# Layer norms by token tile, and a feed-forward net's first unit by token tile

## The reference, cut to what matters

```python
for l in range(DEPTH):                       # DEPTH = 2, ALPHA = (2 * DEPTH) ** 0.25
    x = layer_norm(ALPHA * x + 0.5 * swiglu(x, ffn_w1[l, 0], ffn_w2[l, 0]), ln_g[l, 0], ln_b[l, 0])
    mix = hybrid_mixer(x, ...)
    x = layer_norm(ALPHA * x + mix, ln_g[l, 1], ln_b[l, 1])
    x = layer_norm(ALPHA * x + 0.5 * swiglu(x, ffn_w1[l, 1], ffn_w2[l, 1]), ln_g[l, 2], ln_b[l, 2])

def layer_norm(x, g, b):
    mu = mean(x);  var = mean((x - mu) ** 2)
    return (x - mu) * rsqrt(var + 1e-5) * g + b

def swiglu(x, w1, w2):                       # w1: 1024 x 5632, w2: 2816 x 1024
    g, u = split(x @ w1, 2)
    return (silu(g) * u) @ w2
```

## Time and profile before

| | us |
|---|---|
| time before, median of 3 runs | 1828.71 (1828.14 to 1828.81) |
| the profiled execution | 1828.23 |
| its span (first to last instruction) | 1826.2 |

### The profile page before, as it was taken

One profiled execution on the slowest core, in us unless ns is written; L12 is line 12 of the kernel. 1 busy time (PEld: TensorE's weight loads), 2 busy tenths in 40 slices (PEclk: granted clock), 3 DMA queues, 4 the chain that ended last, 5 costly groups with the idle time before them and its releaser, 6 DMA issues.

```text
span 1826.2 us, 27995 instructions
## 1 busy us (share of the span) xinstructions
PE 1779.8 (97%) x10838; PEld 1567.5 (86%) x10838; DVE 1386.7 (76%) x1543; ACT 989.5 (54%) x953; POOL 60.0 (3%) x99
## 2 busy tenths in 40 slices
PE   9999999999999999999999999999999889999998
PEld 8888899998888888888999988888899668787786
DVE  7655786857778775557868577887768878879988
ACT  6555465633544454444655335444433636869984
POOL 1000000000000000000000000000100010000001
PEclk9999999999999999999999999999999899999999
DMA  7555454564677655554555637775534009989994
GB/s 264 202 192 198 156 179 175 187 252 139 231 276 269 237 184 184 185 194 152 187 186 198 233 124 262 264 286 198 174 116 139 24 8 355 365 323 398 423 381 173
DMA packets 58423, 395.79 MB, mean 217 GB/s; under 512 B 7016, under 2 KB 7392, under 8 KB 12752
## 3 DMA queue, kind: packets, MB, share of 16 engines
q1 hardware_dynamic: 48800, 350.31, 52.8%
q0 software_dynamic: 9504, 44.00, 7.3%
q10 hardware_dynamic: 16, 0.01, 0.0%
HBM read 386.94 MB, written 7.36 MB: 216 GB/s over the span
## 4 chain that ended last, share of the span: by engine, by line
PE 73%; DVE 15%; ACT 4%; issue 3%; DVEq 3%; ACTq 1%; DMA 0%; SPq 0%
PE ps L2207 14%; PE ps L2191 7%; PE ps L2193 7%; PE ps L2192 7%; PE ps L2206 7%; PE ps L2307 3%; PE ps L2308 3%; PE ps L2311 3%; DVE wlo L2670 3%; DVE wlo L1743 2%; PE ps L2204 2%; DVE mod L2798 2%; PE ps L990 2%; PE ps L992 1%; PE ps L991 1%
## 5 line engine op out<-in xcount | busy, mean ns | idle before, releaser
L2670 DVE TENSOR_TENSOR wlo<-raw,whi 128x2048 fp32r<-128x2048 f32 x235 | 536.0, 2290 | 188.5 <-ACT whi L2495 186.4
L2495 ACT ACTIVATE whi<-raw 128x2048 fp32r<-128x2048 f32 x235 | 449.3, 1912 | 279.2 <-PE ps L2193 104.0
L2207 PE MATMUL ps<-xT,whi 128*128 128x512 f32 x1232 | 439.4, 396 | 0.0
L2206 PE MATMUL ps<-xT,wlo 128*128 128x256 f32 x1232 | 344.0, 279 | 0.0
L2207 PEld LDWEIGHTS ps<-xT,whi 128*128 128x128 f32 x1232 | 231.2, 188 | 47.5
L2191 PE MATMUL ps<-xT,whi 128*128 128x256 f32 x912 | 258.2, 283 | 0.0
L2192 PE MATMUL ps<-xT,whi 128*128 128x256 f32 x912 | 258.1, 283 | 0.0
L2193 PE MATMUL ps<-xT,wlo 128*128 128x256 f32 x912 | 258.1, 283 | 0.0
L2206 PEld LDWEIGHTS ps<-xT,wlo 128*128 128x128 f32 x1232 | 232.3, 189 | 8.8 <-DVE xT L2689 1.0
L2519 ACT ACTIVATE rest<-ps 128x512 f32<-128x512 f32 x88 | 52.8, 600 | 241.8 <-PE ps L2207 241.8
L2191 PEld LDWEIGHTS ps<-xT,whi 128*128 128x128 f32 x912 | 175.1, 192 | 0.0
(11 more groups left out here) (589 smaller groups left out, 3358.9 us busy)
## 6 DMA issues: line engine op xcount, KB each, us to landing
raw<-stream SPq DMA_DIRECT2D x236, 1024.0 KB, 4.8
raw<-experts SPq DMA_DIRECT2D x64, 1024.0 KB, 7.7
mod<-experts SPq DMA_DIRECT2D x32, 1024.0 KB, 7.6
adaraw<-ada POOLq DMA_DIRECT2D x24, 1024.0 KB, 5.1
yd<-lnrow POOLq DMA_DIRECT2D x7, 512.0 KB, 6.9
lnrow<-ln_g POOLq DMA_DIRECT2D x6, 512.0 KB, 4.7
lnrow<-ln_b POOLq DMA_DIRECT2D x6, 512.0 KB, 7.2
yd<-lnrow POOLq DMA_DIRECT2D x10, 256.0 KB, 6.5
```

The source lines that it names most:

```text
L2206: nc.tensor.matmul(bank(b, T), wl, xThi[:, k, :], start=False, stop=False)
L2207: return nc.tensor.matmul(bank(b), wh, both, start=False, stop=k == KD - 1)
L2495: act_fn(whi[:, slot, :], raw[:, slot, :], ACT.Copy).then_inc(hi_done, 1)
L2670: v.tensor_tensor(wlo[:, slot, :], raw[:, slot, :], whi[:, slot, :].bitcast(F32), ALU.subtract).then_inc(lo_done, 1)
```

## The change

The norm does all its steps for tile 0, then all for tile 1, with a root of its own for each tile; `mv_done` and `std_done` count tiles. `PIECES` becomes [(0, 0), (0, 1), (1, 0), (1, 1)]. In the norms ahead of a net the low parts of the first two pieces stand behind the two sums of tile 1. ScalarE loads its square root table ahead of the norm and takes one root per tile; between the tiles it splits the weight unit that it split ahead of the norm before; VectorE's weight splits stay behind the norm. In the last step of a net, hidden values are made, split and counted by tile, so `hid_done` and `hlo_done` count one more per net, and `last_rows` waits by tile and always takes the third bank late. `first_unit` multiplies all chunks for tile 0, then for tile 1, with products of 256 and 128 columns, and four fillers between. `first_turned_unit` turns the two pieces of tile 0, runs ten fillers, and begins its products after the third piece. The fillers right behind `last_rows` are gone.

```diff
-NORM_FILL, MERGE_FILL, H1_FILL, H1_TURN_FILL, H2_FILL, TURN_FILL = 20, 18, 25, 8, 17, 5
+MIX_FILL, TILE_FILL, H1_FILL, H1_TURN_FILL, H2_FILL, TURN_FILL = 10, 4, 25, 8, 17, 5
...
-        PIECES = [(0, 0), (1, 0), (0, 1), (1, 1)]
+        PIECES = [(0, 0), (0, 1), (1, 0), (1, 1)]
...
+            def tile_product(slot, tile, k, b, i):
+                c = k * 256 + tile * P
+                wh, wl = whi[:, slot, c:c + P], wlo[:, slot, c:c + P]
+                sl = slice(i * P, (i + 1) * P)
+                both = bank(b).rearrange("p (a t) -> p a t", t=T)[:, :, sl]
+                low = bank(b, T + i * P, T + (i + 1) * P)
+                if k == 0:
+                    nc.tensor.matmul(both, wh, xT[:, k, :, sl], start=True, stop=False)
+                    return nc.tensor.matmul(low, wl, xThi[:, k, sl], start=False, stop=False)
+                nc.tensor.matmul(low, wl, xThi[:, k, sl], start=False, stop=False)
+                return nc.tensor.matmul(both, wh, xT[:, k, :, sl], start=False, stop=k == KD - 1)
...
             def first_unit(rnd, slot, n):
-                for j in range(3):
-                    turn_piece(n, j)
-                for half in range(2):
-                    pe.wait_ge(xTlo_done, n * 4 + (2 * half + 2))
-                    if half == 0:
-                        weights_ready(rnd, slot)
-                    for tile in range(2):
-                        for k in range(4 * half, 4 * half + 4):
-                            last = wide_product(slot, tile, k, tile)
-                        if (half, tile) == (0, 0):
-                            turn_piece(n, 3)
+                turn_piece(n, 0)
+                turn_piece(n, 1)
+                weights_ready(rnd, slot)
+                for i in range(TT):
+                    if i == 1:
+                        keep_busy(TILE_FILL)
+                        turn_piece(n, 2)
+                        turn_piece(n, 3)
+                    for half in range(2):
+                        pe.wait_ge(xTlo_done, n * 4 + (2 * i + half + 1))
+                        for tile in range(2):
+                            for k in range(4 * half, 4 * half + 4):
+                                last = tile_product(slot, tile, k, tile, i)
                 last.then_inc(used, 1)
...
             def first_turned_unit(rnd, slot, b, n):
-                for j in range(3):
-                    turn_piece(n, j)
-                pe.wait_ge(xThi_done, n * 4 + 2)
+                turn_piece(n, 0)
+                turn_piece(n, 1)
+                keep_busy(MIX_FILL)
+                turn_piece(n, 2)
+                pe.wait_ge(xThi_done, n * 4 + 3)
                 weights_ready(rnd, slot)
                 high_products(slot, 0, range(4), outs[0], False)
                 turn_piece(n, 3)
...
             (last_rows)
-                    if bank_no == 0:
+                    if bank_no % 2 == 0:
                         weights_ready(rnd, slot)
-                        pe.wait_ge(*before[j])
+                        pe.wait_ge(*before[j][i])
...
-                if third_first:
-                    part(0, 2)
...
             (ScalarE, at a norm; split_piece is one turn of the old split_stream)
-                norm(l * 3)
-                split_stream(l * 3 + 1)
+            def split_stream(n, base, o):
+                norm_root(n - 1, 0)
+                split_piece(n, 0)
+                split_piece(n, 1)
+                turn(base, o)
+                norm_root(n - 1, 1)
+                split_piece(n, 2)
+                split_piece(n, 3)
...
             (VectorE, norm)
+                def root(i):
+                    dve.wait_ge(std_done, n * TT + i + 1)
+                    v.reciprocal(rstd[:, i, :], std[:, i, :])
+                    dve.drain()
+                    v.tensor_scalar(newt[:, i:i + 1], rstd[:, i, :], rstd[:, i, 0:1], var[:, i, 0:1], ALU.mult, ALU.mult)
+                    dve.drain()
+                    v.scalar_tensor_tensor(rstd[:, i, :], newt[:, i:i + 1], 1.5, rstd[:, i, :], ALU.add, ALU.mult)
+                    dve.drain()
+
+                def normed(i):
+                    moments(i).then_inc(mv_done, 1)
+                    dve.drain()
+                    v.tensor_scalar(var[:, i, :], mv[:, i, 1:2], LN_EPS, -0.5, ALU.add, ALU.mult)
+                    ...
+                    centred(i, 0)
+                    last = centred(i, 1)
+                    ...
+                    root(i)
+                    for h in range(2):
+                        ins = scaled(i, h)
+                        if then != "block2":
+                            ins.then_inc(x_done, 1)
+
                 summed(0, 0)
                 summed(0, 1)
+                normed(0)
                 summed(1, 0)
+                if then == "ffn":
+                    stream_lo(n + 1, 0)
                 summed(1, 1)
+                if then == "ffn":
+                    stream_lo(n + 1, 1)
+                normed(1)
...
             (VectorE, last_step of a net; high is banks 2 and 3, first part)
+                    def tile_hidden(i):
+                        sl = slice(i * P, (i + 1) * P)
+                        ...
+                        v.tensor_tensor(hid[:, 0, :, sl], high[:, :, sl], rest[:, 1, :, sl], ALU.add)
+                        dve.drain()
+                        v.scalar_tensor_tensor(hid[:, 0, :, sl], sil[:, :, sl], 0.5, hid[:, 0, :, sl], ALU.mult,
+                                               ALU.mult).then_inc(hid_done, 1)
+                    ...
+                    tile_hidden(0)
+                    tile_hidden(1)
+                    tile_lo(0)
+                    tile_lo(1)
```

More of the change, by code:

```diff
@@ L2315, in rows_unit, with last_rows @@
                 last.then_inc(used, 1)
-            def last_rows(units, parts, before, third_first):
+            def last_rows(units, parts, before):
                 def part(j, bank_no):
@@ L2337, in last_rows @@
                 part(0, 1)
-                if third_first:
-                    part(0, 2)
                 part(1, 0).then_inc(y0_done, 1)
                 part(1, 1).then_inc(y0_done, 1)
-                if not third_first:
-                    part(0, 2)
+                part(0, 2)
                 part(1, 2).then_inc(y0_done, 1)
@@ L2430, in _ @@
                 ffn(lay, l * 2, l * 3)
-                keep_busy(NORM_FILL)
                 for hf in range(2):
@@ L2751, in norm @@
-                centred(1, 0)
-                dve.drain()
-                dve.wait_ge(std_done, n + 1)
-                v.reciprocal(rstd[:, :, 0], std[:, :, 0])
-                dve.drain()
-                for i in range(TT):
-                    v.tensor_scalar(newt[:, i:i + 1], rstd[:, i, :], rstd[:, i, 0:1], var[:, i, 0:1], ALU.mult, ALU.mult)
-                dve.drain()
-                v.scalar_tensor_tensor(rstd[:, :, 0], newt[:, 0:TT], 1.5, rstd[:, :, 0], ALU.add, ALU.mult)
-                dve.drain()
+                if then == "ffn":
+                    stream_lo(n + 1, 1)
@@ L2773, in norm @@
                     return
-                def piece(j):
-                    scaled(*PIECES[j]).then_inc(x_done, 1)
-                for j in range(3):
-                    piece(j)
-                if then == "ffn":
-                    stream_lo(n + 1, 0)
-                    stream_lo(n + 1, 1)
-                centred(1, 1)
-                dve.drain()
-                piece(3)
                 for j in range(2 if then == "ffn" else 0, 4):
@@ L2812, in ffn, with last_step, tile_lo @@
                     beside(0, True)
+                def last_step(alone):
+                    count = (f + 1) * FFN_STEPS
+                    turn(base, UNITS_FFN - 5)
+                    gate_sum(count)
+                    turn(base, UNITS_FFN - 4)
+                    if not alone:
+                        beside(FFN_STEPS - 1, False)
+                    high = banks(2, 2).rearrange("p (c part t) -> p c part t", part=2, t=T)[:, :, 0, :]
+                    def tile_hidden(i):
+                        sl = slice(i * P, (i + 1) * P)
+                        if i == 0:
+                            dve.wait_ge(rest_done, 2 * count)
+                            dve.wait_ge(silu_done, count)
+                        v.tensor_tensor(hid[:, 0, :, sl], high[:, :, sl], rest[:, 1, :, sl], ALU.add)
+                        dve.drain()
+                        v.scalar_tensor_tensor(hid[:, 0, :, sl], sil[:, :, sl], 0.5, hid[:, 0, :, sl], ALU.mult,
+                                               ALU.mult).then_inc(hid_done, 1)
+                    def tile_lo(i):
+                        sl = slice(i * P, (i + 1) * P)
+                        dve.wait_ge(hhi_done, count + f + i)
+                        v.tensor_tensor(hlo[:, 0, :, sl], hid[:, 0, :, sl], hhi[:, 0, :, sl].bitcast(F32),
+                                        ALU.subtract).then_inc(hlo_done, 1)
+                    tile_hidden(0)
+                    tile_hidden(1)
```

(5 more changed lines are left out.)

149 lines of the change are left out of this document (82 added, 67 removed).

## The result

The changed kernel took 1834.55 us, the median of 7 runs (1833.65 to 1837.09); the kernel before took 1828.81 on the same chip (7 runs, 1828.14 to 1830.31). The ratio is 1.0031, with an interval from 1.0019 to 1.0043: slower by 5.7 us. The forecast was 1830.6 with a range of 1826 to 1838. The likeliest case fell short. What came was the first rival, the clock that falls ahead of the mixers.

The account below looks back on a forecast made before the run. TensorE, busy 97% of the span, was taken as the bound, with VectorE late around the norms. Terms 2.2 + 0.3 + 0.2 - 0.8 = +1.9 us gave 1830.1 us profiled, 1830.6 as median; range 1826 to 1838.

Parts of the forecast that it names:

- likeliest case: Whole kernel: the summed terms hold and the clock stays up, 1830.6 us (1828 to 1833), chance 46%.
- the first rival: Ahead of the mixers: the clock falls in a 4.5 us pause; 1832.4 to 1839 us, middle 1834.6, chance 20%.
- The price of a fall: Ahead of a mixer: slow products at the low clock cost 0.9 to 4.3 us per fall, middle 2.
- Norms 0 and 3: Net to mixer: the third piece of x comes later and VectorE ends later, +1.1 us each, 2.2 in all.
- TensorE's +1.3: Mixer's first product, norms 0 and 3: starts 1.3 us later, but this disappears in TensorE's wait for `xclo`.
- the fourth turns come 8 products later: Norms 0 and 3: the fourth piece's turns follow eight products, 0.95 us, in the chain to VectorE's end at 208.0.
- Norms 1 and 4: Merge to net: unit 0 ends at 459.35 instead of 459.79, a gain of 0.4 us each, 0.8 in all.
- Narrow products: Nets' first unit, second tile: an fp32r product of 128 columns takes 0.118 us, 32 products 3.8 us.
- The rival at 0.24: Norms 1, 2 and 4: narrow products cost 0.24 us, 2.9 us more in each norm, 1839.3 us; chance 18%.
- Norm 2: Net to net: no wait to cover, unit 0 ends at 653.6 against 653.27, +0.3 us.
- Norm 5: Ahead of block 2: one more root and `var`, less the drains and 0.1 at the start, +0.2 us.
- The last step by tile: Nets ahead of norms 0, 2, 3, 5: six half-width instructions of 0.43 us, the norm starts 0.1 us earlier.

Follow-up runs that it names:

- merge_only: By tile only in norms 1 and 4 with the by-tile first unit behind them, all else as in the kernel before: 1827.08 us.
- a_fill24: The changed kernel with 24 instead of 10 fillers between the turned tiles ahead of a mixer: 1831.06 us.
- mixer_only: The change only in norms 0 and 3 and those nets' last steps, with 24 fillers, the other norms as in the kernel before: 1831.16 us.
- turn4: a_fill24 with the fourth piece turned right behind the third instead of behind the first unit's first eight products: 1828.52 us.
- early3: The changed kernel with 24 fillers and, in norms 0 and 3, the third piece of x scaled ahead of tile 1's last centred half: 1832.80 us.
- early3b: early3 with 19 instead of 24 fillers ahead of the mixers, and with the fillers of fill_all in the nets' first unit: 1829.63 us.
- whole_last: a_fill24 with the last step of each net whole instead of by tile: 1833.05 us, the median of six runs.
- fill_all: a_fill24 with fillers in the nets' first unit too (five, five instead of four, and two): 1831.10 us.
- b_gap: The kernel before with 12 instead of 20 fillers ahead of the two mixers, order of the norm unchanged: 1829.01 us.
- merge_last: merge_only with all four nets' last steps by tile and fillers in the nets' first unit: 1827.29 us.

## Why the prediction was right or wrong

**The clock.** Here the likeliest case failed. It said that the clock stays up; the rival had 20%. The rival's place and rows were right: after ten fillers the pauses were 3.11 and 0.69 us around four turns, the 4.5 us that I had set between a pause that did nothing and one of 5.4 us that did. I gave it one chance in five because 4.5 lay between, when the nearer of the two was the one with a fall. And the pause that I held against it is no evidence. TensorE stands 2.03 us there, up to 1427.94, in the kernel before, and the clock stayed up; it stands as long at that place in all 13 other traces, and in 8 of them the clock falls right behind it, in the changed kernel too. The kernel before, then merge_only, where the clock was low from 1427.2 to 1430.7:

```profile
1427.94 1.16 PE L883 MATMUL ps<-qkT 64*128 64x128 f32 x16 [2.03 <-ACT qkT L1192]
```

```profile
1426.86 1.75 PE L889 MATMUL ps<-qkT 64*128 64x128 f32 x16 [2.03 <-ACT qkT L1198]
```

One trace without a fall does not show that a pause is harmless. The price of a fall was set at 0.9 to 4.3 us, middle 2. Measured are 1.3 and 1.2 in the traces: near the lower end, which was the price of the eight slow products ahead of the last piece alone. The low clock lasted 6.8 us at norm 0, close to the 8 taken from the rows, and 3.4 at norm 3. What the products behind the last piece cost did not reach the time, since the `xclo` wait took it up.

**Norms 0 and 3.** Forecast +1.1 each, that is 1.2 after the norm's start. With the clock kept it is 1.74 and 1.36 (a_fill24), and +2.5 for both with the last steps' gain (mixer_only) against 2.2. The chain itself was sized well: VectorE's norm 0 takes 17.79 us in a_fill24, 17.34 without its pause, and 17.25 was forecast. What failed is the comparison. The 16.06 us of the earlier trace rows hold a pause of 0.46 us for which my chain by tile, built from the pauseless, had no counterpart. I counted that pause as saved without knowing it. In norm 3 it is (1.36), in norm 0 it came back at another instruction (1.74). The rows of the kernel before that I had not looked at, the first of them with ScalarE's root ahead of it, which was there by 198.8, so that VectorE did not wait for it:

```profile
198.47 0.30 ACT L2533 ACTIVATE std<-mv,eps 128x2 f32<-128x2 f32 x1 [0.40 <-DVE mv L2729]
```

```profile
199.81 0.17 DVE L2754 RECIPROCAL rstd<-std 128x2 f32<-128x2 f32 x1 [0.46 <-issue]
```

```profile
833.43 0.21 DVE L2729 BATCH_NORM_AGGREGATE mv<-stats 128x2 f32<-128x12 f32 x1 [0.44 <-issue]
```

That VectorE's end counts and TensorE's +1.3 disappears was right, and turn4 shows it. And the step "the fourth turns come 8 products later" named the 1.26 us that could be had back, and I took it as given. With the turn moved the new order costs 0.40 and 0.01 us a mixer.

**Norms 1 and 4.** Forecast -0.4 each, measured -0.43 to -0.45 in the traces without a fall or a pause of VectorE there, and with them alone the time fell by 1.2, of which 0.37 is the pause in norm 3. Chain, wait and products came out one by one. Where a pause of 0.45 us fell into norm 4 (early3, early3b, whole_last), less than 0.1 of the gain was left.

**Narrow products.** Forecast 0.118 us each, and 3.8 us for 32: measured 3.8. The rival at 0.24 is ruled out. Its record was the right thing to look at: one record for an fp32r product against two for a plain one.

**Norm 2.** +0.3 forecast, +0.28 measured.

**Norm 5.** +0.2 forecast, +0.74 measured. Of it, 0.43 is another pause of VectorE, and the sums of `mod`, which wait for the second tile's statistics, started 0.69 us after TensorE was free for them:

```profile
1278.22 0.16 DVE L2793 SCALAR_TENSOR_TENSOR rstd<-newt,rstd 128x1 f32<-128x1 f32 x1 [0.43 <-issue]
```

```profile
1282.92 7.13 PE L703 MATMUL ps<-mod,ones 128*128 128x512 f32 x16 [0.69 <-DVE mv L2776]
```

**The last step by tile.** Half width was 0.43 forecast, 0.42 and 0.43 measured; six of them and a wait of 0.34. The gain is 0.14 us for a net against the kernel before (5.82 for 5.96 us from the last rows to the first sum), 0.1 forecast.

**Block 2.** +0.8 us that no step has. The windows 1400 to 1460 have a mean clock of 0.89 (before 0.91) and 1460 to 1560 one of 0.98 (before 1.00). In fill_all, with a like VectorE, the span is 3.3 longer and block 2 begins 3.2 later, so it is no part of the change. In the changed kernel's execution the clock was low twice more in block 2, for 3.4 us each, at 1433.3 and 1508.4; the last 400 us took 0.86 us longer than before, and in a_fill24, without those two, 0.26 less than before. The kernel before varies in the same way: of its 96 executions beside the experiments, the 57 with a mean clock of 0.997 have medians 0.4 to 1.0 us below those of the 39 at 0.995 or 0.996 in each group. When a pause ends in a fall and when not is open.

**The sum.** Without the clock it was +1.9 against +2.7 (a_fill24) and +2.3 (fill_all). Short by 0.4 to 0.8; the pauses in norm 0 and norm 5, 0.45 and 0.43, are about that much. So the rival's 1834.6 met the measured 1834.55 by luck: it was made of 1.9 us and two falls of 2.0, and came as 2.7 us, two falls of 1.3 and 1.2, and about half a us more, most likely the clock in block 2.

## What to carry to other kernels

Fillers that look like waste are the price of the clock: where a change takes them out or widens the pause beside them, count TensorE's standing time up to the next dense stretch, compare it with the shortest stretch that ended in a low clock in any trace at hand, and treat "close to it" as a fall; a single trace in which the clock stayed up clears no pause. When one operand's pieces arrive in a new order, look again at every instruction that was queued between them for the old order: a turn that stood behind eight products, because its piece used to come late, was here half of the loss. Put fillers in each pause before you compare versions that differ by a few tenths of a per cent, since otherwise the falls decide.

## What the runs showed of the hardware

A short stretch at 1.2 GHz does not always follow the same pause. In kernels with eight turns, 1.35 us of nothing and then narrow products, the clock stayed up in some executions and fell in others (changed kernel and a_fill24: up; early3, turn4 and whole_last: down in one or two of the nets). A pause of 2.03 us in block 2 was followed by a fall in 8 of 14 traces. The low clock lasted 3.4 us in some places (norm 3 of the changed kernel, b_gap, turn4, early3 behind norm 2), 6.8 in others (norm 0 of the changed kernel, early3 behind norm 1, whole_last), and up to 10.2 in block 2.

VectorE pauses for 0.26 to 0.46 us, mostly 0.43 to 0.46, once to three times in the norms of a trace, waiting for nothing that the profile shows. The place goes with VectorE's own code. The changed kernel, a_fill24, turn4 and fill_all, whose VectorE code is the same, all pause in norm 0 at the second instruction (0.45 us) and in norm 5 at the first tile's `rstd` (0.43); the kernel before pauses in norm 0 at the root (0.46) and in norm 3 at an aggregation (0.44), and merge_last in norms 0, 4 and 5. Counted along VectorE's records in a trace, from 0, the pauses keep to fixed numbers more than to instructions: one stands at 217, in norm 0, in all 13 traces other than that of the kernel before, one at 1553 or 1554, in norm 5, in 11 of them, and others 128 apart from it (1297, 1425, 1681, 1809). Behind 48 of the 108 pauses over 0.25 us, a packet of 8192 bytes starts 0.5 to 0.95 us later on the queue that the page calls `q14 instruction`, which has some 30 such packets in a whole trace. That speaks for the loading of VectorE's code as their cause, but no run tested it. Either way, an edit of VectorE's code moves these pauses onto the path or off it, and that is 0.4 us which no count of instructions gives.

An fp32r product of 128 columns lets the next one start after 0.06 to 0.07 us, and the 256-column one behind it takes 0.17: a pair takes 0.23 us, as long as two products of 256 columns at 0.118. In both streams the weight loads start 0.10 to 0.13 us apart; that they set the pace is not shown.
